# A two-layer hybrid decoder step on one core: expert passes of 108 rows, meta tokens left out of the experts, and the value and time-step columns of w_in in one slab

## What is computed

```python
x += w_out @ [ SSD(h) | RMSNorm(SWA(h)) ],   h = RMSNorm(x)
logits = h @ w_router;  top_v, top_i = top_k(logits, 2);  gates = softmax(top_v)
out[t] = sum over the 2 experts e of t:  gates * (silu(h @ wg[e]) * (h @ wu[e])) @ wd[e]
return xp[:, N_META:], xs, ...          # no output holds the last x of a meta token
```

## Time and profile before

| | us |
|---|---|
| median of 3 runs | 1642.56 |
| the three runs | 1647.07, 1642.56, 1642.11 |
| the profiled execution | 1647.14 |
| its span, first to last instruction | 1645.0 |

### The profile page before, as it was taken

How to read it: one execution, slowest core, us unless ns; L and a number is a source line. 1 busy time by engine, 2 the same in 40 slices (tenths; PEclk the granted TensorE clock), 3 DMA queues, 4 the chain that set the end, 5 groups by cost and what they waited for, 6 DMA issues and landing times.

```text
span 1645.0 us, 44685 instructions
## 1 busy us (share of the span) xinstructions
PE 1602.7 (97%) x20702; PEld 1352.5 (82%) x20702; DVE 283.4 (17%) x673; ACT 202.9 (12%) x527; POOL 131.7 (8%) x202
## 2 busy tenths in 40 slices
PE   7999999999999999999899999999999999999998
PEld 5666666666666666765899999999999999999897
DVE  2354630000000235453200000000000000000021
ACT  1244310000000024522000000000000000000000
POOL 3221116000000011111100000000000000000100
PEclk9999989999999899999899999999999999999999
DMA  9923237994333323223699999999999999999991
GB/s 278 240 70 93 69 117 200 364 304 170 114 125 106 90 80 93 68 73 127 215 355 340 344 349 337 358 345 345 348 341 349 345 341 355 338 356 343 349 340 35
DMA packets 192292, 395.21 MB, mean 240 GB/s; under 512 B 9698, under 2 KB 63578, under 8 KB 191952
## 3 DMA queue, kind: packets, MB, share of 16 engines
q1 hardware_dynamic: 176560, 346.31, 62.6%
q0 software_dynamic: 15168, 45.95, 9.1%
q10 hardware_dynamic: 384, 0.13, 0.0%
HBM read 357.23 MB, written 37.09 MB: 240 GB/s over the span
## 4 chain that ended last, share of the span: by engine, by line
PE 96%; DVE 2%; issue 1%; ACT 1%; DMA 0%; SPq 0%; DVEq 0%; ACTq 0%
PE bank L1306 33%; PE bank L1328 16%; PE bank L1218 12%; PE bank L751 6%; PE bank L1235 6%; PE bank L1054 3%; PE bank L734 2%; PE bank L1071 2%; PE bank L719 1%; PE bank L705 1%; PE bank L1027 1%; PE bank L1038 1%; PE bank L722 1%; PE bank L987 1%; PE bank L1044 1%
## 5 line engine op out<-in xcount | busy, mean ns | idle before, releaser
L1306 PE MATMUL bank<-arena,ring 128*64 128x112 f32 x11264 | 549.5, 260 | 6.8 <-issue 6.1
L1306 PEld LDWEIGHTS bank<-arena,ring 128*64 128x64 f32 x11264 | 545.0, 138 | 11.0 <-issue 8.9
L1328 PE MATMUL bank<-arena,ring 128*64 128x112 f32 x5632 | 271.6, 259 | 0.0
L1328 PEld LDWEIGHTS bank<-arena,ring 128*64 128x64 f32 x5632 | 270.6, 137 | 0.1
L1218 PE MATMUL bank<-hnT,ring 128*128 128x336 f32 x704 | 200.6, 449 | 1.8 <-DVE hnT L1673 1.8
L1218 PEld LDWEIGHTS bank<-hnT,ring 128*128 128x128 f32 x704 | 134.5, 191 | 67.9 <-issue 3.0
L751 PE MATMUL bank<-hnT,ring 128*128 128x336 f32 x384 | 119.8, 457 | 0.0
L2120 DVE TENSOR_TENSOR arena<-arena,bank 128x448 f32<-128x448 f32 (+1 forms) x48 | 27.9, 582 | 519.4 <-PE bank L1306 519.4
L1235 PE MATMUL bank<-arena,ring 128*128 128x336 f32 x352 | 99.6, 446 | 0.0
L751 PEld LDWEIGHTS bank<-hnT,ring 128*128 128x128 f32 x384 | 70.7, 192 | 34.9 <-issue 6.8
L1235 PEld LDWEIGHTS bank<-arena,ring 128*128 128x128 f32 x352 | 66.9, 190 | 32.6
(11 more groups left out here) (359 smaller groups left out, 1106.5 us busy)
## 6 DMA issues: line engine op xcount, KB each, us to landing
ring<-in_moe_w_gate SPq DMA_DIRECT2D x88, 1024.0 KB, 5.9
ring<-in_moe_w_up SPq DMA_DIRECT2D x88, 1024.0 KB, 6.1
ring<-in_moe_w_down SPq DMA_DIRECT2D x88, 1024.0 KB, 5.7
ring<-in_w_in SPq DMA_DIRECT2D x18, 1024.0 KB, 7.5
ring<-in_w_gate SPq DMA_DIRECT2D x11, 1024.0 KB, 10.6
ring<-in_w_up SPq DMA_DIRECT2D x11, 1024.0 KB, 12.5
xg_rows<-arena POOLq DMA_DIRECT2D x1, 11200.0 KB, 51.2
y_rows<-arena POOLq DMA_DIRECT2D x1, 10752.0 KB, 92.4
```

Of the source, the lines that this page charges most:

```text
L1306: ins = mm(into[rows, SLOTS * fi:SLOTS * fi + SLOTS], weights[:, c, col:col + 64], xg[:, k0 + c, :], start=(k0 + c == 0 and fi == 0), stop ...
L1328: ins = mm(bank[5 + c // 4][rows, SLOTS * (c % 4):SLOTS * (c % 4) + SLOTS], weights[:, col:col + 64], hid[:, f, :], start=(f == 0 and c % ...
```

## The change

1. `SLOTS` becomes 108. Everything sized by it follows: the streamed columns of the expert matmuls, the rows of a block, the evictions. `PASSES` is now counted from the 320 tokens that are routed and stays 3. `y_rows` gets one more block of rows.
2. The 16 meta tokens get no expert. Their two expert numbers are raised by 16, so that no comparison with 0 to 7 is true for them, and their rows in `xg_rows` and `y_rows` are 32 rows of the extra block (`aside`).
3. `w_in` has 10 slabs instead of 9. The first holds 128 value columns and 8 time-step columns side by side for each of the 8 row groups, the second the keys. One group of matmuls streams 136 columns, instead of one of 128 and one of 8; `load_wdt` is gone. The constants' transfer keeps its place behind the query slabs.

```diff
-SLOTS = 112
-PASSES = -(-NT // SLOTS)
+SLOTS = 108
+ROUTED = NT - META
+PASSES = -(-ROUTED // SLOTS)
-IN_SLABS, OUT_SLABS = 9, 4
+IN_SLABS, OUT_SLABS = 10, 4
...
-    slabs = [cols(w, 2056)]
+    rows = w.rearrange("(k p) n -> p k n", p=128)
+    slabs = [[(whole, lambda s: s[:, 0:DK * 136].rearrange("p (k n) -> p k n", k=DK)[:, :, 0:128], rows[:, :, 2184:2312]),
+              (whole, lambda s: s[:, 0:DK * 136].rearrange("p (k n) -> p k n", k=DK)[:, :, 128:136], rows[:, :, 1536:1544])],
+             [(whole, lambda s: s[:, 0:DK * 128].rearrange("p (k n) -> p k n", k=DK), rows[:, :, 2056:2184])]]
...
-                def load_wdt(l):
-                    pool.dma_start(wdt, a["w_in"][l][:, 1536:1544].rearrange("(k p) n -> p k n", p=128)).then_inc(dtw_here, 16)
...
-                pe.wait_ge(dtw_here, 16 * (l + 1))
...
                 wait_slab(pe, s0)
+                vdt = slab(s0)[:, 0:DK * 136].rearrange("p (k n) -> p k n", k=DK)
                 for i, (t0, n) in enumerate(TILES):
                     for k in range(DK):
                         if i == 0:
                             pe.wait_ge(hn_ready, 8 * 2 * l + k + 1)
-                        mm(bank[1][0:n, 128 * i:128 * i + 128], hnT[:, k, t0:t0 + n], sl(0)[:, k, 128:256], start=(k == 0), stop=(k == DK - 1))
-                for i, (t0, n) in enumerate(TILES):
-                    for k in range(DK):
-                        ins = mm(bank[1][0:n, 384 + 8 * i:392 + 8 * i], hnT[:, k, t0:t0 + n], wdt[:, k, :], start=(k == 0), stop=(k == DK - 1))
+                        ins = mm(bank[1][0:n, 136 * i:136 * i + 136], hnT[:, k, t0:t0 + n], vdt[:, k, :], start=(k == 0), stop=(k == DK - 1))
                 ins.then_inc(proj_psum, 1)
-                column_chunk(bank[2][:, 0:NT], sl(0), 0).then_inc(proj_psum, 1)
+                owed[0] += 1
+                wait_slab(pe, s0 + 1)
+                column_chunk(bank[2][:, 0:NT], slab(s0 + 1)[:, 0:DK * 128].rearrange("p (k n) -> p k n", k=DK), 0).then_inc(proj_psum, 1)
...
             link(v.memset(route[:, 0:400], 0.0))
+            nowhere, aside, is_meta = route[:, 392:393], route[:, 393:395], upper[:, UOFF[0] + META - 1:UOFF[0] + META]
+            v.tensor_scalar(nowhere, is_meta, float(2 * EXPERTS), None, ALU.mult)
+            link(v.tensor_tensor(route[:, 300:316], ident[:, 0:META], iota[:, 0:META], ALU.mult))
+            link(v.tensor_reduce(route[:, 395:396], route[:, 300:316], AX.X, ALU.add))
+            for c in range(2):
+                ins = v.tensor_scalar(aside[:, c:c + 1], is_meta, float(PASSES * EXPERTS * SLOTS + META * c), route[:, 395:396], ALU.mult, ALU.add)
+            link(ins)
...
-            link(v.tensor_copy(which, idx[:, :, 0:2]))
+            v.tensor_scalar(which[:, 0, :], idx[:, 0, 0:2], nowhere, None, ALU.add)
+            link(v.tensor_copy(which[:, 1:3, :], idx[:, 1:3, 0:2]))
...
+            link(v.tensor_tensor(route[:, 384:386], route[:, 384:386], aside, ALU.add))
```

27 lines of the change are left out of this document (13 added, 14 removed).

## The result

The changed kernel took 1602.45 us, the median of 4 runs (1593.97 to 1604.01), beside 1644.45 for the kernel before in the same session (4 runs, 1642.11 to 1647.07): a ratio of **0.9737**, 95% interval 0.9711 to 0.9763, so 2.6% faster. The forecast was 1598.5, with a range of 1593 to 1608. In terms of the profiled executions, which the sum was made in, it is closer: 1647.14 before, 1603.16 after, 44.0 us less, where the sum said 44.1.

A forecast was written before the change was run, and what follows sets the result against it. TensorE was taken to bound the kernel, experts included. 28.6 + 0.35 + 11.25 - 0.65 + 4.8 - 0.2 = 44.1 us saved, from the median of 1642.6 giving 1598.5 us, range 1593 to 1608.

The forecast's parts named there:

- Experts, 28.6 us: Expert gate, up and down matmuls: 4 columns fewer at 0.423 ns each, over 16896 instructions, save 28.6 us.
- Rival A: Experts: weight loads, not streamed columns, set the pace, so the 28.6 us falls away: 1627 us; chance 0.04.
- Time-step matmuls, 11.25: Mixers: the 48 8-column matmuls per layer go, saving 6.18 us in layer 0 and 5.07 in layer 1.
- 136 columns, 0.65: Mixers: the 96 value matmuls grow by 8 columns at 0.85 ns each, costing 0.65 us.
- The clock behind them, 4.8: Key matmuls in both layers: without 8-column matmuls before them the clock stays at 2.4 GHz, saving 4.8 us.
- Rival B: Mixers: the clock falls anyway, where L719 waits for DVE column by column: 1603.3 us; chance 0.2.
- Routing, 0.2: Routing: one more small DVE operation on the way to the expert counts, where TensorE waits, costs 0.2 us.
- the gather: The 48 matmuls gathering the first expert's rows, with 56 row transposes, lose 4 columns each, saving 0.35 us.
- Copies at 0: Dense FFN: blank copies of 108 rows cost nothing; landings of 49.4 us would become 66 on 12 engines.
- the cover of 91 us: Dense FFN: the slab ring's lead, at 9.1 us a slab; landings below 91 us were to cost nothing.
- The 0.01 that I gave to it: Dense FFN: chance 0.01 that slabs behind the 12-engine copies come later than 91 us, making the kernel slower.
- rival C: Experts: DMA becomes the bound at 347 GB/s, giving 1602 us; 373 GB/s seen elsewhere spoke against it; chance 0.1.

The follow-up runs named there:

- the expert part alone: The kernel before with SLOTS = 108 and meta tokens routed to no expert, w_in slabs and mixers left as they were: 1619.92 us, ratio 0.9861.
- filler: The changed kernel plus eight unread 336-column matmuls where TensorE waits in the routing: 1604.26 us, 0.9809 of the kernel before.

## Why the prediction was right, and where it was not

**Experts, 28.6 us:** 821.1 - 792.5 = 28.6 in busy time, to the tenth, and that is luck in part: with the expert part alone it was 26.4, and the stretch from the first to the last expert matmul shrank by 26.8 between the means of three executions with 112 rows and five with 108. So the price of a column is right, and the term about 2 us high. In the first pair of executions the stretch gave 30.4; the kernel before had stood idle for 2.7 us soon after the start of its first expert, in four pieces of this row's kind:

```profile
797.37 0.41 PE L1306 MATMUL bank<-arena,ring 128*64 128x112 f32 x4 [0.94 <-issue]
```

I had read no more than 6.1 us of issue waits in the earlier trace rows and asked nothing of them. Rival A (weight loads pace the stream) is out: at 100 columns with half the bytes an instruction took 733.2 us / 16896 = 43.4 ns. The Trainium skill's 53 ns for such a load (TensorE: Matmul & The Clock Gate, section LDWEIGHTS) is not what this stream is bound by.

**Time-step matmuls, 11.25, and 136 columns, 0.65:** L718 takes 7.3 us to the start of L703 in both layers, 152 ns an instruction and not the 115 I named under what would show it; that was a slip, since L719 took 7.12 us to the start of L722 in layer 0, 148 ns, already. The eight columns cost 0.2 us there, where I had 0.3.

**The clock behind them, 4.8:** L703 to L732 is 4.61 us in each layer, against 6.44 and 7.61: 4.83. Together the mixers gave 7.83 + 8.93 = 16.8 us, against 11.25 - 0.65 + 4.8 = 15.4: the half clock within the values of layer 1 was gone as well. That was this execution: in the changed kernel's other two it was there again (544.99 to 548.41 us in the second), and the mixers gave 15.2 and 15.7. Rival B is out only as to its price. The clock does fall in the thin stretch of values: in layer 0 in five of the eleven executions with the wide group, in layer 1 in eight. But it is up again before the keys, and costs 0.3 to 0.5 us in layer 0 and 0.6 to 1.1 in layer 1, not 4.8.

**Routing, 0.2:** 0.13. But the **clock in the routing and the gather** is the step that was missing. I took the gather as 48 matmuls that get 0.35 us cheaper, partly with the transposes; they became 3.3 us dearer. The kernel before already had the clock at 0.50 from 778.6 to 788.8 us, through half of the gather, so this was to be asked. The changed kernel's other two profiled executions lost 0.7 and 1.9 us there, so it is partly a matter of the execution. But not only: from the gather's start to the first expert matmul it was 8.0 to 8.4 us in the three kernels with 112 rows, and 11.2 or 11.3 in seven of the nine executions with fewer rows and no filler. Why the expert part brings this was not tested. Of the 3.95 us between forecast and median, 1.9 are the median of before, which a fourth run moved from 1642.56 to 1644.45; the rest lies inside the spread of the four executions after, and I assign it to no single term. The terms themselves came to 39.9 to 42.0 us by medians, not 44.1; the experts and the gather, each some 2 us, are where the traces show it.

**Copies at 0, landings of 66 us by the Trainium skill** (the section named above): the sum was right, and what I made of the rule was not. The blank copies did get slower (51.2 to 71.8 us, 92.4 to 113.0), but slabs issued from 300 to 345 us landed in 34.8 to 44.2 us, not in 66 (with the expert part alone the slowest took 58.5). A copy on fewer engines takes longer itself and, as far as the rule holds, leaves the others to the slabs. I had not seen how near the edge was: 104 rows and eight more blocks, and TensorE waited 26 us. Nor was the cover of 91 us the right one: the slowest landing there was 82.5, and TensorE waited all the same. The slabs it stood for landed at 371.6, 383.4, 391.7, 413.1 and 434.8 us, 16 us apart on average, where it uses one in 9.1; so what counts there is the rate at which slabs come, and not the delay of one. The 0.01 that I gave to it belonged to a real mechanism, one step of the same kind away.

**DMA, rival C:** 357 GB/s and no slab late, so it is out. My cover of 373 GB/s was for the wrong thing, though. The question was not whether the weights arrive but what else shares their engines, and at 108 columns the change was already close to what that allows: the next four columns returned a third of their price. Whether the 2 us missing at 108 have the same cause stays open: gaps in step with a packet are 2 to 8 there and 1 before, but the idle put down to "issue" did not grow (6.1 us before, 4.6 after).

## What to carry to other kernels

A linear price such as ns per column holds until another resource paces the stream, and with DMA engines at a share of 1.00 that resource need not be the data: look at idle time put down to "issue", and whether it comes at a fixed number of instructions. When a size changes, look at every transfer whose outer dimension it is: 108, 104 and 100 in place of 112 made the same copies much slower, and writing them from 128 rows cost nothing. And fold matmuls of a few columns into wide ones rather than moving them about.

## What the runs showed of the hardware that I had not expected

- At 353 to 373 GB/s of traffic (104 and 100 rows), TensorE pauses for up to 2.4 us at places 128 matmuls with 128 weight loads, or a multiple, apart, in step with 16 KB packets on the instruction queue, while the weights land in 6.4 us. Halving the traffic ended it (28.6 us of issue waits to 4.1) and sped up the same stream by 38.5 us in 786.9.
- A blank copy of 13.7 MB landed in 177.6 us from 104 rows, the same volume in 92.6 us from 128.
- The same values and time steps ran at 2.4 GHz in one layer and mostly at 1.2 GHz, for 17.1 us, in the other, in one execution; and one kernel's routing had 13.6 to 23.9 us at 1.2 GHz from one execution to the next.
